# Two blocks with routed experts on one core: where squares, gelu and silu are computed in the second block, and how the routing and the bias rows are prepared in the first

## The reference

```python
def moe_ffn(...):                       # first block
    logits = xt @ w_router + b_router
    top_vals, top_idx = lax.top_k(logits, 4)
    top_gates = softmax(top_vals)
    # for each expert e, on the rows of the tokens that chose it (blocks of 128):
    gate = minimum(xb @ w_gate[e] + b_gate[e], 7)
    up = clip(xb @ w_up[e] + b_up[e], -7, 7)
    y = (gate * sigmoid(1.702 * gate) * (up + 1)) @ w_down[e] + b_down[e]

def second_block(...):
    q, k, v, z_a, u_b, v_b, z_b, g_a, g_b = split(rmsnorm(x) @ w_in)
    y_a = stick_breaking_attention(q, k, v) * silu(z_a)
    vn = layernorm(gelu(v_b), groups of 64) * ln_g + ln_b
    y_b = gelu(u_b) * (w_spatial @ vn + b_spatial) * silu(z_b)
    merged = sigmoid(g_a) * (y_a @ w_up_a) + sigmoid(g_b) * (y_b @ w_up_b)
    x = x + merged @ w_out
```

## Time and profile before

| | |
|---|---|
| median of 3 runs | 1929.27 us (1928.42 to 1931.82) |
| profiled execution | 1927.19 us, its span 1925.9 us |
| PE busy | 1841.0 us (96%) |
| DVE busy | 1426.3 us (74%) |
| ACT busy | 1180.6 us (61%) |
| POOL busy | 215.8 us (11%) |
| mean granted TensorE clock | 0.972 of 2.4 GHz |

### The profile page before, as it was taken

The page is one execution under the profiler, slowest core; times in us unless marked ns, Lnnn a source line. Parts: engine busy times, 40 slices in busy tenths (PEclk is TensorE's granted clock), DMA queues, the critical chain, the costliest instruction groups (busy, mean ns, idle before and its releaser), DMA issues.

```text
span 1925.9 us, 20815 instructions
## 1 busy us (share of the span) xinstructions
PE 1841.0 (96%) x8267; PEld 1454.0 (75%) x8267; DVE 1426.3 (74%) x1228; ACT 1180.6 (61%) x882; POOL 215.8 (11%) x133
## 2 busy tenths in 40 slices
PE   7999858999999999999999999999998999999998
PEld 5777747878888888878878878888864876668876
DVE  4466668989989989989989989989957334464342
ACT  4353346777777777777777777777753255672221
POOL 1311410211211211211211211111000000000000
PEclk9999869999999999999999999999998999899999
DMA  7321437999999999999999999999966311112221
GB/s 251 110 76 51 137 146 286 349 369 359 357 374 359 359 374 358 358 367 358 353 372 357 355 372 359 356 374 362 352 250 248 102 51 66 44 50 88 88 77 44
DMA packets 95042, 487.16 MB, mean 253 GB/s; under 512 B 13832, under 2 KB 15408, under 8 KB 44768
## 3 DMA queue, kind: packets, MB, share of 16 engines
q1 hardware_dynamic: 81120, 462.64, 64.3%
q0 software_dynamic: 9520, 17.13, 2.4%
q10 hardware_dynamic: 4304, 6.03, 1.0%
HBM read 481.56 MB, written 20.97 MB: 261 GB/s over the span
## 4 chain that ended last, share of the span: by engine, by line
PE 88%; DVE 6%; ACT 3%; issue 1%; DMA 1%; POOL 0%; SPq 0%; ACTq 0%; DVEq 0%; POOLq 0%
PE PS L448 81%; PE PS L680 3%; DVE WL L1230 2%; PE PS L860 1%; PE PS L848 1%; ACT WH L913 1%; PE PS L841 1%; DMA ring<-in_w_in_dram 1%; DVE HV L1241 0%; PE PS L480 0%; DMA xg<-h2d,tok 0%; PE PS L558 0%; PE PS L880 0%; DVE X L1241 0%; DVE Pp L1615 0%
## 5 line engine op out<-in xcount | busy, mean ns | idle before, releaser
L1230 DVE TENSOR_TENSOR WL<-ring,WH 128x2048 fp32r<-128x2048 f32 x428 | 971.4, 2295 | 279.8 <-ACT WH L913 279.7
L913 ACT ACTIVATE WH<-ring 128x2048 fp32r<-128x2048 f32 x428 | 816.3, 1916 | 394.9 <-PE PS L448 394.7
L448 PE MATMUL PS<-WH,xh 128*128 128x512 f32 x1024 | 332.5, 406 | 2.4 <-DVE xl L1469 2.4
L448 PE MATMUL PS<-WL,xh 128*128 128x512 f32 x1024 | 320.8, 394 | 0.0
L448 PE MATMUL PS<-WH,xl 128*128 128x512 f32 x1024 | 320.1, 394 | 0.0
L448 PEld LDWEIGHTS PS<-WL,xh 128*128 128x128 f32 x1024 | 193.2, 189 | 44.5
L448 PEld LDWEIGHTS PS<-WH,xl 128*128 128x128 f32 x1024 | 192.9, 188 | 44.4
L448 PEld LDWEIGHTS PS<-WH,xh 128*128 128x128 f32 x1024 | 189.3, 190 | 43.4 <-DVE xl L1469 2.8
L1779 POOL DMA_INDIRECT yd<-ys,dst x32 | 65.4, 2045 | 993.2 <-ACT ys L1071 993.2
L448 PE MATMUL PS<-WH,hh 128*128 128x512 f32 x512 | 163.5, 400 | 2.6 <-DVE hl L1469 2.6
L448 PE MATMUL PS<-WH,hl 128*128 128x512 f32 x512 | 160.5, 394 | 0.0
(11 more groups left out here) (346 smaller groups left out, 2193.8 us busy)
## 6 DMA issues: line engine op xcount, KB each, us to landing
ring<-in_w_gate_dram SPq DMA_DIRECT2D x128, 1024.0 KB, 7.4
ring<-in_w_up_dram SPq DMA_DIRECT2D x128, 1024.0 KB, 7.1
ring<-in_w_down_dram SPq DMA_DIRECT2D x128, 1024.0 KB, 8.2
ring<-in_w_in_dram SPq DMA_DIRECT2D x32, 1024.0 KB, 5.3
ring<-in_w_out_dram SPq DMA_DIRECT2D x8, 1024.0 KB, 5.0
yk<-yd SPq DMA_DIRECT2D x6, 1024.0 KB, 7.2
X<-in_x_dram SPq DMA_DIRECT2D x4, 512.0 KB, 9.8
h2d<-HV ACTq DMA_DIRECT2D x4, 512.0 KB, 2.7
```

What stands on the lines that cost most here:

```text
L448: return P.matmul(ps, a, b, start=start, stop=stop)
L913: A.activation(WH[buf[n]], ring[spot[n]], ACT.Copy).then_inc(s_hi, 1)
L1230: V.tensor_tensor(WL[buf[n]], ring[spot[n]], WH[buf[n]].bitcast(F32), SUB).then_inc(s_lo, 1)
```

## The change

In the second block ACT no longer squares: `centred(j)` on DVE now holds mean, difference, product with itself and sum, and both tiles of a head follow each other behind the head's last copy of a bank. Gelu of `gu`, silu of `zb` and their product stand behind the attention. Silu of z_a is read from PSUM straight into a new tile `za`, which saves DVE four copies. `scaled` moves to heads 5 and 6. In the routing, all four choices are compared in one instruction (`eq`, 128 by 512) and the table is one product and one sum over k. The first three experts get an index each of its own bank, the first before the one-hots of the others, and the first gather waits for that index alone; the count of further blocks comes later. The wait for the zeroed rows is gone from DVE, and POOL zeroes them as soon as the logits are there. The bias rows are two fp32r parts: ACT rounds them, DVE zeroes the third part (32 partitions) and takes the rest; POOL does nothing for them.

```diff
-    b3 = place("b3", [96, 2, D], BF16)
-    sel96 = place("sel96", [96, 32], BF16)
+    sel96 = place("sel96", [96, 32], F32R)
+    b3 = reg("b3", [96, 2, D], F32R, 44)
+    za = place("za", [128, 4, 512], F32, B3)
...
     def spread_out(o, v):
-        for k in range(4):
-            ... eq = (iota == mf[k]);  e2 = eq * v[k];  o = o + e2
+        V.tensor_tensor(e2, eq, v.unsqueeze(2).broadcast_to([128, 4, E, K]), MUL).then_inc(dv.sem, dv.one())
+        V.wait_ge(dv.sem, dv.n)
+        return V.tensor_reduce(o, e2, AX, ADD)
...
 tensor_turn_rows(e)
-        P.wait_ge(s_ix, min(e + NI, E))
+        P.wait_ge(s_ix, min(e + NI, E) if e else 1)
...
 scalar_routing
+        A.wait_ge(s_bst, 48)
+        A.activation(b3[0:32], bst, ACT.Copy).then_inc(s_bh, 1)
...
 scalar_second
-            if h in (3, 4):
-                square(2 * (h - 3))          # and square(2 * (h - 3) + 1) behind the Exp
-            if h == 4:
-                A.activation(gu, gu, ACT.Gelu_apprx_tanh).then_inc(s_gg, 1)
-            if h == 6:
-                A.activation(zb, zb, ACT.Silu).then_inc(s_act, 1)
         for c in range(4):
-            A.activation(zb[:, c], zb[:, c], ACT.Silu).then_inc(s_act, 1)
+            A.wait_ge(s_mm, done[n_za + 1] + c + 1)
+            if c == 2:
+                A.wait_ge(s_val, 8)
+            A.activation(za[:, c], PS[:, c, :], ACT.Silu).then_inc(s_act, 1)
+        A.wait_ge(s_zuzv, 12)
+        A.activation(zb, zb, ACT.Silu)
+        A.activation(gu, gu, ACT.Gelu_apprx_tanh).then_inc(s_gg, 1)
         for c in range(4):
             A.wait_ge(s_yam, c + 1)
+            A.wait_ge(s_zgu, 1)
             A.activation(yah[:, c], ya[:, c], ACT.Copy).then_inc(s_fh, 1)
...
 vector_routing
+        V.wait_ge(s_bh, 1)
+        V.memset(b3[64:96].bitcast(F32), 0.0)
+        V.tensor_tensor(b3[32:64], bst, b3[0:32].bitcast(F32), SUB).then_inc(s_b3, 1)
         V.wait_ge(s_lgt, 4)
         ...
+        V.tensor_tensor(eq, iota, mf[:, :, 0:K], ALU.is_equal).then_inc(dv.sem, dv.one())   # both broadcast
+        spread_out(DV, token numbers)
+        V.tensor_scalar(M16, DV, 0.0, None, ALU.is_gt).then_inc(s_m16, 1)
         ...
+        vector_one_hot(0)
+        vector_index(0, 7)
+        for q in range(1, NI):
+            vector_one_hot(q)
+        for q in range(1, NI):
+            vector_index(q, (4, 5)[q - 1])
...
 vector_second, centred(j)
             V.scalar_tensor_tensor(U[j], wide(s8[:, j, 0:8]), -1.0 / 64, U[j], MUL, ADD)
+            V.tensor_tensor(sq2, U[j], U[j], MUL).then_inc(dv.sem, dv.one())
+            V.tensor_reduce(s8[:, j, 8:16], sq2, AX, ADD).then_inc(s_sv, 1)
...
 vector_second, the heads
-            if h == 7:
-                V.tensor_tensor(gu, gu, zb, MUL).then_inc(s_zgu, 1)
             if h in (3, 4):
-                variance(2 * (h - 3))
-                centred(2 * (h - 3) + 1)
+                for j in (2 * (h - 3), 2 * (h - 3) + 1):
+                    centred(j)
+            if h in (5, 6):
+                for j in (2 * (h - 5), 2 * (h - 5) + 1):
+                    last = scaled(j)
-        for j in (2, 3):
-            last = scaled(j)
 behind the heads
+        V.wait_ge(s_gg, 1)
+        V.tensor_tensor(gu, gu, zb, MUL).then_inc(s_zgu, 1)
...
-    def gpsimd_biases():                     # six instructions of 32x2048 on POOL
 gpsimd_gather(e)
-        G.wait_ge(s_ix, max(NI, e + 1))
+        G.wait_ge(s_ix, e + 1)
 gpsimd_experts
-        G.wait_ge(s_pos, 1)
-        G.wait_ge(s_b3, 1)
+        G.wait_ge(s_lgt, 4)
```

More of the change, by code:

```diff
@@ L168, in program, with routing @@
     tri16 = reg("tri16", [128, 2, 128], F16, 31.5)
[L169 to L182, removed]
+    HV = [reg(f"HV{i}", [128, D], F32, (40, 80.5, 56, 60)[i]) for i in range(4)]
+    row = [B3]
+    def routing(name, shape, dt):
+        size = (int(np.prod(shape[1:])) * 4 + 31) // 32 * 32
+        row[0] += size
+        return place(name, shape, dt, row[0] - size)
+    LG, DV, M, Gt = (routing(n, [128, 4, E], F32) for n in ("LG", "DV", "M", "Gt"))
+    M16 = routing("M16", [128, 4, E], F16)
+    mx, mf = (routing(n, [128, 4, 8], F32) for n in ("mx", "mf"))
+    mi = routing("mi", [128, 4, 8], U32)
+    nm, sm = (routing(n, [128, 4], F32) for n in ("nm", "sm"))
+    eq = reg("eq", [128, 4, E, K], F32, 22)
+    e2 = reg("e2", [128, 4, E, K], F32, 24)
+    b3 = reg("b3", [96, 2, D], F32R, 44)
     bst = reg("bst", [32, 2, D], F32, 64.25)
-    r1 = reg("r1", [32, 2, D], F32, 72.5)
     xg = [reg(f"xg{i}", [128, D], F32, 4 * i) for i in range(2)]
@@ L669, in tensor_routing, with tensor_index @@
         last.then_inc(s_pos, 1)
-    def tensor_index(q, column):
+    def tensor_index(q, bank):
         P.wait_ge(s_oh, q + 1)
         for j in range(4):
-            last = mm(PS[:, 7, column:column + 1], oh[q % NI][:, j], DV16[:, j, q:q + 1], j == 0, j == 3)
+            last = mm(PS[:, bank, 0:1], oh[q % NI][:, j], DV16[:, j, q:q + 1], j == 0, j == 3)
         last.then_inc(s_im, 1)
@@ L748, in tensor_experts @@
     def tensor_experts():
-        P.wait_ge(s_tall, 14)
+        P.wait_ge(s_tall, 16)
         for q in range(NI):
-            tensor_index(q, q)
+            tensor_index(q, (7, 4, 5)[q])
         tensor_turn_rows(0)
@@ L1150, in scalar_second @@
                     A.activation(wsT[:, 4 * hf:4 * hf + 4], PS[:, 4 + hf, :].rearrange("p (g t) -> p g t", g=4), ACT.Copy).then_inc(s_wsk, 1)
[L1152 to L1155, removed]
-            A.activation(sq2, gv[:, j].rearrange("p (g c) -> p g c", g=8), ACT.Square).then_inc(s_sg2, 1)
         for h in range(8):
@@ L1265, in vector_mixer @@
         low(ahead(n_v))
-        for i in range(3):
+        for i in range(2):
             V.tensor_copy(sel96[32 * i:32 * i + 32], C[0:32, IDENT:IDENT + 32])
+        V.tensor_copy(sel96[64:96], C[64:96, IDENT:IDENT + 32])
         low(ahead(n_v + 1))
@@ L1486, in vector_experts @@
     def vector_experts():
[L1487 to L1490, removed]
-        vector_index(0, NI)
+        vector_further_count()
         low(first + NX - 1)
+        V.wait_ge(s_gk, 1)
         spread_out(Gt, GK).then_inc(s_sp, 1)
@@ L1569, in vector_second @@
             low(ahead(n0 + 1))
-        kept = (gv, gu, zb, zb)
+        kept = (gv, gu, zb)
         V.tensor_copy(tri[:, 0], C[:, TRII:TRII + 128])
@@ L1579, in evacuate @@
             for n, kh, c, w in steps:
-                if kh:
+                if kh and w < 3:
                     V.wait_ge(s_mm, done[n] + c + 1)
```

112 lines of the change are left out of this document (40 added, 72 removed).

## The result

The kernel after takes 1895.60 us (median of 4 runs, 1894.78 to 1896.78) against 1928.85 of the kernel before (4 runs, 1927.24 to 1931.82): a ratio of 0.9826, 95% interval 0.9809 to 0.9843. That is 33 us less. Forecast were 31.0 and 1898. The profiled execution took 1894.84 us with a span of 1893.5, 32.4 less than before's.

The account below looks back on a forecast made before the run. PE was taken as the bound nearly everywhere, losing time to stalls and the lowered clock behind them. Terms 14.6 + 6.6 + 3.5 + 6.0 + 0.3 = 31.0 us gave a median of 1898; forecast 1895 to 1902, range 1891 to 1906 (0.82).

Parts of the forecast that it names:

- Heads 3 to 5: Attention: without squares and gelu ahead, all three heads run as plain ones of 18.97 us, gaining 14.6 us; other end 6.6.
- The margin of 1.0 us: Heads 3 and 4: DVE's added 5.8 us of instructions fit its 6.83 us idle gap by 1.0 us.
- Behind head 7: From the last head's end to the next projection: masks done in time, PE goes straight on, gain 6.6 us; lower bound 4.1.
- Routing to the logits: Routing up to the logits: without POOL's bias work DVE's writes shorten, logits 2.8 to 4.7 us earlier, taken as 3.5.
- clock kept: Routing's third tile: at full clock DVE's chain decides, logits 4.7 us earlier; at half clock 2.8.
- Logits to the gather: Routing, logits to first gather: fewer DVE instructions and waits before the first index, gain 6.0 us.
- The gather itself: First gather: weight transfers that shared its time start later against it, gain 0.3 us, kept 0 to 1.4.
- Bias rows: 128 bias matmuls in fp32r instead of bf16: same pitch of 0.234 us, longer loads hidden, cost taken as 0.
- other bound 11.5: Bias rows: all 128 longer weight loads exposed at 0.09 us each, 11.5 us lost, 1909.5 in all; chance 0.05.
- They hide in 0.27 idle: Bias rows: a load 0.09 us longer is hidden in the 0.27 us PEld sat idle before each pair.

Follow-up runs that it names:

- second_only: The kernel before with the second block's edits alone, routing and bias rows as before: 1909.99 us, ratio 0.9895.
- squares_back: The kernel after with the four squares back on ACT in and behind heads 3 and 4, DVE's order restored: 1906.29 us, ratio 0.9889.
- gelu_back: The kernel after with gelu of `gu` back in head 4 and silu of `zb` in head 6, squares left on DVE: 1895.24 us, ratio 0.9819.
- routing_only: The kernel before with the edits of routing and bias rows alone: 1919.32 us, ratio 0.9942.
- pool_busy: The kernel after with POOL's six bias-row instructions back in their old place, results unread: 1900.23 us in a single run.
- after_down128: The kernel after with two small tiles sharing another's place, so the large region lies 128 bytes lower: 1887.52 us, ratio 0.9773.
- after_up64: The kernel after with the large region 64 bytes higher, at the addresses of the kernel before: 1895.57 us, ratio 0.983.
- before_again: The kernel before once more, unchanged, a single run for a second trace: 1931.98 us.
- bias_bf16: The kernel after with bias rows in bf16, third part zero, which also put the large region 64 bytes lower: 1873.30 us, ratio 0.9707.
- after_down64: The kernel after with one 64-byte tile sharing another's place, so the large region lies 64 bytes lower: 1871.70 us, ratio 0.9713.
- even64_memset: From the kernel after with its region 64 bytes lower: every tile 96 bytes higher, bias memset ahead of DVE's wait: 1873.28 us, ratio 0.9708.

## Why the prediction was right, point by point

**Heads 3 to 5** (forecast 14.6, measured 71.53 - 56.40 = 15.1). Right as to place, cause and size: second_only, at before's addresses, needs 57.02 us for them, a gain of 14.5, and squares_back shows the squares as the cause of 9.4. The margin of 1.0 us was 0.96. The heads are 18.80 instead of my 18.97: that is the address, not the change. Of the stage's 14.04 in the table, head 0 gave 1.6 back: its half clock behind a wait of PE of 1.53 us for `PH` (1560.08) is absent in gelu_back and squares_back, which have the same work there and take 18.5 us, while routing_only, pool_busy and after_down128 take 20.0 to 20.1 again; I take it as spread.

**Behind head 7** (6.6, measured 6.90). The masks were done in time, PE went straight on, z_a was read in time, and `yal` was written by 1720.3, 7 us ahead of its need. second_only and squares_back have the same 5.79 us there. Which of the moved instructions (product, copies, `scaled`) gave how much was not taken apart.

**Routing to the logits** (3.5, measured 4.77). The case "clock kept" came about (DVE's chain decides: 4.7 was its price). In after_up64, squares_back and routing_only the clock was lost at this place, and the same stage took 36.73, 36.67 and 36.53: 2.8 to 3.0 less than before's 39.51, and 3.4 to 3.6 less than before_again's 40.09. The step between 2.8 and 4.7 is thus drawn anew by each execution. One reading under this term was wrong: POOL does not make each of DVE's writes 1.0 slower, as I counted, but holds DVE up until its own instruction ends. POOL's timeline of before, beside `HV` (223.62, 2.31) and `WL` (225.92, 3.89), shows it:

```profile
218.81 6.02 POOL L1765 TENSOR_TENSOR bst<-r,bmid 32x2048 f32<-32x2048 f32 x1
224.90 2.77 POOL L1767 CAST b<-bst 32x2048 bf16<-32x2048 f32 x1
```

`HV` ends 1.10 us behind the first and `WL` 2.14 behind the second, as in pool_busy. What POOL costs is a matter of where its instruction ends, and varies: this `HV` took 2.31 us in before and 4.21 in before_again.

**Logits to the gather** (6.0, measured 13.93 - 8.33 = 5.6). Right.

**The gather itself** (0.3, kept 0 to 1.4; measured 7.36 - 4.11 = 3.25). This is the term that was mis-sized, by a factor of ten. I counted a later start of the weights as a small help. In before SP's issues of the next weights (two of 1 MB, from 255.19) fell within the gather, and the DMA engines' share was 0.96 from 257 to 261; in after they begin at 248.49, 0.2 us before PE's turn, and the share during the gather is 0.35. But that is not all of it: the gather's own instruction on POOL took 2.27 us in before (and in second_only), while DVE wrote two `WL`, and 1.14 in after, routing_only and bias_bf16, while DVE ran only short instructions. So 1.1 us passed on POOL, and at most 2.1 are left for the transfers. No run parts the two.

**Bias rows** (0, other bound 11.5; measured 1.5 to 1.9 over 29 of the 32 experts). The load was not hidden wholly. "They hide in 0.27 idle" was argued from the idle time in front of each pair; the second matmul of a pair, or the weights' queue behind it, was left out. Which of these is the place was not tried.

**"Durations of unchanged matmuls carry over"** was never written, and was the greatest mistake that didn't show. The shift of a region by 64 bytes cost 1.2 to 1.5 us in the experts and gave 2.0 to 2.5 back at the end (134.07 or 134.61 to 132.08) and some 0.17 in each head. In the whole this did not show: the medians of after_up64 and after are 1895.57 and 1895.60. Had the same edits shifted it by 128, the time would have been 1872, 19 us below my range, with every step of the argument intact.

**The balance.** By the stages of the table, measured minus forecast gain: heads -0.56, behind head 7 +0.30, to the logits +1.27, to the first expert matmul +2.45 (forecast 6.3), experts -4.64 (3.1 of it the change's, 1.5 spread), the end +3.93, ahead of the routing -1.07, join -0.28. That is +1.40, from 31.0 to 32.4. Of the end's 3.93, 2.53 lie in the 576 matmuls (134.61 to 132.08; at least 2.0 of it the address, by second_only's 134.07), and 1.37 the last 192 matmuls (46.41 to 45.04), which is a draw of the clock (see below). The forecast was right because its terms for the heads, the stretch behind head 7 and the routing were, and right to 2 us by luck: the gather gave 3 us more than counted, and what no term had named (experts, address, clock) cancelled.

## What to carry to other kernels

An instruction that an engine's list has ahead of a due one is worth moving even where it gets no shorter (a square took 0.63 us on ACT, 0.69 on DVE), if the other engine idles there: measure that idle gap first. Before timing any edit that adds, drops or resizes a small tile, note where the large tiles start, and compare at equal addresses; and try a few shifts of 32 to 128 bytes by themselves, since one was worth 22 to 24 us here, seven tenths of the whole change. after_down64 is the fastest of all kernels here: the change plus one tile moved, 1871.70 us.

## What the runs showed of the hardware

- The pitch of the 512-column fp32r matmuls depends on where the large region lies in SBUF: 576 of them take 130.80, 132.08 or 134.1 to 134.6 us by 64-byte shifts of the region, 130.80 in all three kernels with region and first weight buffers alike, 132.07 or 132.08 in all six with after's addresses.
- The granted clock after a wait is no fixed thing. Behind the same idle time of 2.20 us ahead of the last 192 matmuls, it stayed at 2.4 GHz in after and fell to 1.2 GHz behind the first matmul in gelu_back, with the same addresses: 45.04 against 46.59 us. Such a draw is worth 1.6 us. The first two experts (59.07 in before, 60.66 in second_only) and the third tile of the routing (2.25 and 2.24 us of idle time, clock kept in after and lost in even64_memset) show two more; a comparison of stages has to leave them out.

The line of gelu_back, beside after's that stands above:

```profile
1837.87 46.59 PE PS L441 x192
```

- PE had the rows of a gather of 128 rows 4.1 us after its issue on DMA engines at a share of 0.35, and 7.4 us after it where two weight transfers of 1 MB were issued meanwhile and DVE wrote `WL`; 1.1 of the difference passed on POOL itself.
- An instruction of DVE that meets one of POOL's on SBUF ended 1.1 us (`HV`) or 2.1 us (`WL`) behind the end of POOL's, in before as in pool_busy.
